# Seven ring places in the output stage, diagonals in place of scaled rows, and a final gain applied slice by slice, in a two-block fp32 transformer kernel

## What is computed

```python
h_l = modulate(rms_norm(x, norm1_w), sh1, sc1)
g_a, g_b = split(sigmoid(h @ w_gate + b_gate), 2)
mix_l = (g_a * (ya @ w_proj_gla) + g_b * (yb @ w_proj_diff)) @ w_out
x_new = x + g1 * mix_l
h2_l = modulate(rms_norm(x_new, norm2_w), sh2, sc2)
x_new = x_new + g2 * conv_ffn(h2_l, w_up, conv_w, conv_b, w_down)
```

## Time and profile before

| what | value |
|---|---|
| runs | 2488.26, 2486.78, 2485.66 us; median 2486.78 |
| profiled execution | 2486.4 us, its span 2484.4 us |
| granted TensorE clock, mean | 0.972 |
| busy: TensorE matmul / weight load | 2363.7 us (95%) / 2074.9 us (84%) |
| busy: VectorE / ScalarE | 1464.6 us (59%) / 1056.2 us (43%) |
| DMA | 456.46 MB, mean 184 GB/s |

### The profile page before, as it was taken

One profiled execution on the slowest core, in us unless ns is written; L12 is line 12 of the kernel. 1 busy time (PEld: TensorE's weight loads), 2 busy tenths in 40 slices (PEclk: granted clock), 3 DMA queues, 4 the chain that ended last, 5 costly groups with the idle time before them and its releaser, 6 DMA issues.

```text
span 2484.4 us, 37594 instructions
## 1 busy us (share of the span) xinstructions
PE 2363.7 (95%) x15615; PEld 2074.9 (84%) x15615; DVE 1464.6 (59%) x2035; ACT 1056.2 (43%) x1435; POOL 43.4 (2%) x53
## 2 busy tenths in 40 slices
PE   5779899999999998898999999999999999999997
PEld 1346787799988998778999988999978999998876
DVE  1124666649567567766888754566766543276654
ACT  3223333345456552335444433444454443254433
POOL 2000000002000000000000000000000000000000
PEclk8889999999999999999999999999999999899999
DMA  9664576645444467775877756666655566244454
GB/s 312 212 206 136 178 220 213 194 136 147 129 145 128 133 208 251 259 241 149 253 243 252 234 189 190 186 180 185 186 164 189 166 192 189 74 130 119 111 174 147
DMA packets 255433, 456.46 MB, mean 184 GB/s; under 512 B 20947, under 2 KB 49937, under 8 KB 254112
## 3 DMA queue, kind: packets, MB, share of 16 engines
q1 hardware_dynamic: 252672, 442.47, 58.0%
q0 software_dynamic: 2016, 7.40, 0.8%
q10 hardware_dynamic: 576, 4.19, 0.4%
HBM read 451.91 MB, written 2.10 MB: 183 GB/s over the span
## 4 chain that ended last, share of the span: by engine, by line
PE 84%; DMA 5%; DVE 5%; ACT 3%; issue 1%; DVEq 1%; ACTq 0%; SPq 0%
PE psum L595 73%; DMA sbuf<-in_w_ada 2%; PE psum L662 2%; PE psum L572 2%; DVE fast L1844 2%; ACT fast L1246 1%; PE psum L1099 1%; DVE sbuf L1892 1%; DMA sbuf<-in_w_proj_diff 1%; DMA sbuf<-in_w_out 1%; PE psum L843 1%; DMA sbuf<-in_w_proj_gla 1%; PE psum L898 1%; PE psum L1129 1%; PE psum L917 1%
## 5 line engine op out<-in xcount | busy, mean ns | idle before, releaser
L595 PE MATMUL psum<-fast,fast 128*128 128x256 f32 (+3 forms) x13680 | 2084.9, 314 | 40.2 <-DVE fast L1844 32.8
L595 PEld LDWEIGHTS psum<-fast,fast 128*128 128x128 f32 (+2 forms) x13680 | 1893.0, 191 | 219.3 <-issue 47.7
L1844 DVE TENSOR_TENSOR fast<-sbuf,fast 128x1024 fp32r<-128x1024 f32 (+3 forms) x655 | 781.4, 1197 | 791.5 <-ACT fast L1246 783.7
L1246 ACT ACTIVATE fast<-sbuf 128x1024 fp32r<-128x1024 f32 (+3 forms) x659 | 678.8, 1034 | 1080.1 <-PE psum L595 918.3
L1892 DVE SCALAR_TENSOR_TENSOR sbuf<-sbuf,sbuf 128x512 f32<-128x512 f32 x240 | 180.4, 752 | 21.6 <-DMA sbuf<-in_w_ada 1.5
L1246 ACT ACTIVATE sbuf<-psum 128x512 f32<-128x512 f32 (+5 forms) x216 | 99.6, 484 | 190.0 <-PE psum L662 90.4
L662 PE MATMUL psum<-sbuf 128*32 128x512 f32 x256 | 70.6, 738 | 27.5 <-DMA sbuf<-in_w_ada 27.4
L572 PE MATMUL psum<-sbuf,sbuf 128*128 128x128 f32 (+2 forms) x317 | 56.9, 291 | 22.2 <-DMA sbuf<-in_consts 10.2
L572 PEld LDWEIGHTS psum<-sbuf,sbuf 128*128 128x128 f32 (+2 forms) x317 | 38.9, 147 | 44.6 <-issue 15.0
L662 PEld LDWEIGHTS psum<-sbuf 128*32 128x32 f32 x256 | 9.8, 118 | 69.3 <-DMA sbuf<-in_w_ada 58.4
L1864 DVE TENSOR_TENSOR fast<-sbuf,fast 128x512 fp32r<-128x512 f32 (+1 forms) x61 | 53.4, 876 | 4.6
(11 more groups left out here) (246 smaller groups left out, 967.7 us busy)
## 6 DMA issues: line engine op xcount, KB each, us to landing
sbuf<-in_w_ada SPq DMA_DIRECT2D x192, 512.0 KB, 4.7
sbuf<-in_w_up SPq DMA_DIRECT2D x176, 512.0 KB, 4.0
sbuf<-in_w_in SPq DMA_DIRECT2D x158, 512.0 KB, 3.9
sbuf<-in_w_down SPq DMA_DIRECT2D x88, 512.0 KB, 4.4
sbuf<-in_w_gate SPq DMA_DIRECT2D x64, 512.0 KB, 3.7
sbuf<-in_w_out SPq DMA_DIRECT2D x64, 512.0 KB, 4.8
sbuf<-in_w_proj_gla SPq DMA_DIRECT2D x16, 512.0 KB, 4.9
sbuf<-in_w_proj_diff SPq DMA_DIRECT2D x16, 512.0 KB, 5.6
```

The source lines that it names most:

```text
L595: last = mm(out, lhsT, rhs, start=first and key not in opened, stop=end, skip_group_check=True)
L1246: return A(out, in_, ACT.Copy, scale=scale)
L1844: last = tt(lo, raw, hi.bitcast(F32), ALU.subtract)
```

## The change

1. **Ring.** Besides the four places, three more exist for the chunks from gate7's first to uv1's last, at M_Y + 18080, 19104 and 21152. Each chunk takes the place that was used least recently. The first load into a new place waits for `diff_pv_done` = 8.
2. **Rows turned by a diagonal.** `rows_scale` goes. `row_scales` multiplies the identity (128 x 128) by the column of factors, once for each half of the rows; `turn_unit` uses these two diagonals as moving operand of an ordinary matmul, with x1 (or the memory rows) unscaled. The scaled copy `xs` goes.
3. **Logarithm early.** Before the last squares of out3, downb3 and o23, ScalarE computes a logarithm of one column that nobody reads.
4. **The end.** In each of the four slices VectorE multiplies x by the gain (two operations of 128 x 512); after `rsqrt`, VectorE scales the first 128 rows and ScalarE the other 128, in four pieces each. The stores keep their order and wait for the engine that makes the piece.

```diff
+EXTRA = [("gate7", "uv1", [18080, 19104, 21152], ("diff_pv_done", 8))]
...
+        self.places = [(0, len(self.chunks), M_RAW + SLOT_WORDS * s, None) for s in range(SLOTS)]
+        for first, final, offsets, free in EXTRA:
+            self.places += [(self.job[first][0], self.job[final][-1] + 1, M_Y + at, free) for at in offsets]
+        self.place, self.earlier, self.loads = [], [], []
+        users = [[] for _ in self.places]
+        for g in range(len(self.chunks)):
+            s = min((n for n, (a, b, _, _) in enumerate(self.places) if a <= g < b),
+                    key=lambda n: users[n][-1] if users[n] else -1)
+            self.place.append(s)
+            self.earlier.append(users[s][-1] if users[s] else None)
+            users[s].append(g)
+            self.loads.append(len(users[s]))
...
-        xs = Y(13984, 2, D)
+        scales = Y(6144, 2, P)
...
-                if g >= SLOTS:
-                    name, count = st.released(g - SLOTS)
+                if st.earlier[g] is not None:
+                    name, count = st.released(st.earlier[g])
+                    sp.wait_ge(S(name), count)
+                elif st.places[st.place[g]][3]:
+                    name, count = st.places[st.place[g]][3]
                     sp.wait_ge(S(name), count)
...
-                sp.wait_ge(S("out_ready"), n + 1)
+                sp.wait_ge(S(f"out_scaled{n % 2}"), n // 2 + 1)
...
             def turn_unit(name, src, u, before):
-                pe.wait_ge(S(f"{name}_rows_scaled"), u // 2 + 1)
+                pe.wait_ge(S(f"{name}_scales_ready"), 1)
...
-                        last = transposed(bank(4 + u % 4, j * T + t * P, P), src[t][:, k * P:(k + 1) * P])
+                        last = mm(bank(4 + u % 4, j * T + t * P, P), src[t][:, k * P:(k + 1) * P], scales[:, t, :],
+                                  start=True, stop=True)
...
+            def logarithms_next():
+                A(small[:, 84:85], small[:, 7:8], ACT.Ln)
...
             rsqrt(small[:, 58:60])
+            act.drain()
+            for n in range(4):
+                act.wait_ge(S("rows_gained"), 2 * n + 2)
+                c = slice(512 * n, 512 * n + 512)
+                copy(onat[:, 1, c], onat[:, 1, c], small[:, 59:60]).then_inc(S("out_scaled1"), 1)
...
-            def rows_scale(name, dst, src, rs):
+            def row_scales(name, rs, earlier=None):
                 rsqrt_wait()
-                for c in range(0, D, 512):
-                    for t in range(2):
-                        last = ts(dst[t][:, c:c + 512], src[t][:, c:c + 512], small[:, rs + t:rs + t + 1], None, ALU.mult)
-                    last.then_inc(S(f"{name}_rows_scaled"), 1)
-                    yield
+                if earlier:
+                    dve.wait_ge(S(f"{earlier}_turned"), 8)
+                for t in range(2):
+                    last = ts(scales[:, t, :], C("ident"), small[:, rs + t:rs + t + 1], None, ALU.mult)
+                last.then_inc(S(f"{name}_scales_ready"), 1)
...
                     stt(x1[:, t, c], src, 0.5, x1[:, t, c], ALU.mult, ALU.add).then_inc(emptied, 1)
+                dve.drain()
+                dve.wait_ge(S("gain_loaded"), 16)
+                for t in range(2):
+                    tt(onat[:, t, c], x1[:, t, c], fgb[:, c], ALU.mult).then_inc(S("rows_gained"), 1)
             row_variance(48, 4, ("x1_squared", 24))
             rsqrt_wait()
-            dve.wait_ge(S("gain_loaded"), 16)
             for n in range(4):
                 c = slice(512 * n, 512 * n + 512)
-                for t in range(2):
-                    stt(onat[:, t, c], x1[:, t, c], small[:, 58 + t:59 + t], fgb[:, c], ALU.mult, ALU.mult
-                        ).then_inc(S("out_ready"), 1)
+                ts(onat[:, 0, c], onat[:, 0, c], small[:, 58:59], None, ALU.mult).then_inc(S("out_scaled0"), 1)
```

More of the change, by code:

```diff
@@ L256, in landed @@
     def landed(self, g):
-        return f"slot_loaded{g % SLOTS}", 16 * (g // SLOTS + 1)
+        return f"slot_loaded{self.place[g]}", 16 * self.loads[g]
     def released(self, g):
@@ L358, in ring @@
             w, row, kt, kp, col, width = st.chunks[g]
-            s = g % SLOTS
-            return area(M_RAW + s * SLOT_WORDS, SLOT_WORDS)[0:kp, 0:kt * width].rearrange("p (k n) -> p k n", k=kt)
+            return area(st.places[st.place[g]][2], SLOT_WORDS)[0:kp, 0:kt * width].rearrange("p (k n) -> p k n", k=kt)
         def half(g, part):
@@ L991, in turn_unit @@
                         k = 2 * u + j
-                        last = transposed(bank(4 + u % 4, j * T + t * P, P), src[t][:, k * P:(k + 1) * P])
+                        last = mm(bank(4 + u % 4, j * T + t * P, P), src[t][:, k * P:(k + 1) * P], scales[:, t, :],
+                                  start=True, stop=True)
                 last.then_inc(S(f"{name}_turned"), 1)
-            xsT = [xs[:, 0, :], xs[:, 1, :]]
+            x1T = [x1[:, 0, :], x1[:, 1, :]]
             pe.wait_ge(S("g1_kept"), 4)
             for u in range(4):
-                turn_unit("norm2", xsT, u, 0)
+                turn_unit("norm2", x1T, u, 0)
             def norm2_chunk(q):
@@ L1002, in norm2_chunk @@
                 if q >= 1 and q + 3 < 8:
-                    turn_unit("norm2", xsT, q + 3, 0)
+                    turn_unit("norm2", x1T, q + 3, 0)
             def up(i):
@@ L1040, in norm3_units @@
                 for u in range(8):
-                    turn_unit("norm3", xsT, u, 16)
+                    turn_unit("norm3", x1T, u, 16)
                     yield
@@ L1599, in squares @@
                       ).then_inc(S("x1_squared"), 1)
+            def logarithms_next():
+                A(small[:, 84:85], small[:, 7:8], ACT.Ln)
             for n in range(4):
                 steps(f"out{n}")
+                if n == 3:
+                    logarithms_next()
                 squares(0, n)
@@ L2221, in unit @@
                 split_values(hi, lo, X[:, lc, 1, 2 * u:2 * u + 2, :]).then_inc(S(f"{name}_ready"), 1)
-            x1T, xsT = ([x[:, 0, :], x[:, 1, :]] for x in (x1, xs))
             row_variance(48, 4, ("x1_squared", 8))
[L2225 to L2232, removed]
+            row_scales("norm2", 58)
+            for u in range(3):
+                unit("norm2", u, 0, 0)
             def taps(s, i, b):
@@ L2302, in mem_units @@
                 yield
[L2303 to L2306, removed]
+                row_scales("mem", 66, "norm2")
+                for _ in range(7):
+                    yield
                 for u in range(8):
@@ L2318, in norm3_units @@
                 row_variance(48, 4, ("x1_squared", 16))
-                scaling = rows_scale("norm3", xsT, x1T, 58)
                 yield
[L2321 to L2326, removed]
+                row_scales("norm3", 58, "mem")
+                yield
+                for u in range(8):
                     yield
```

## The result

The changed kernel takes 2472.87 us (median of 7 runs, 2468.39 to 2480.11); the kernel before took 2488.15 us on the same chip (7 runs). The ratio is 0.9938, 95% interval 0.9924 to 0.9953: faster by 15 us where 28 were forecast, and 4 us above the upper end of the range. The profiled execution took 2468.4 us with a span of 2466.3 us.

What follows compares the result with a forecast made beforehand. The output stage was held by the latency of a four-place ring, not bandwidth. Gains 25.0 + (0.4 + 1.2 + 0.4) + 0.8 + 0.5 = 28.3 us off 2486.4 gave 2458.1, forecast as 2458.5 us; range 2450 to 2469.

Steps and rivals of the forecast that it cites:

- The diagonals: Turns at norm2, mem and norm3: an fp32 product takes 0.11 us like a transpose, so cost zero.
- rival of more passes: Turns: an fp32 matmul takes twice a transpose, adding 10.6 us over 96 operations, 2469 us in all; chance 0.04.
- The ring: Output stage (pg, pd, out): three more places for weight loads end most waits, 25.0 us gained.
- floor: pd: VectorE's work without its waits for ScalarE allows no less than 49.9 us; 51 was taken.
- the delay behind each panel's end: out: additions and ScalarE's squares after every job delay the next split, 1.7 us in all.
- The 2 us set aside for bursts: Output stage: stalls that remain while loads of x and memory rows compete, 2 us (0 to 11).
- The rival of bursts: Output stage: bursts and late splits keep a third of the stalls, 19 us gained in all, 2468 us; chance 0.18.
- Places idle: Ring: release order leaves the new places unused, only 3.3 us gained, 2483.5 us; chance 0.03.
- slower by SyncE's wait: gate7: SyncE's queue waits for the eighth `diff_pv_done`, holding all loads; for instance 2497 us; chance 0.03.
- Scalings: VectorE's spared scalings shorten TensorE's waits: 0.4 us at norm2, 1.2 at mem, 0.4 at norm3.
- Logarithm early: norm2: the table load moves into ScalarE's wait for the additions, 0.8 us gained; 0 at norm3.
- The end: Last slice: the first store goes out 0.5 us earlier; the stores' DMA time still ends last.

Runs made afterwards that it cites:

- e3: The kernel before with only the row scaling replaced by diagonals: 2497.07 us, ratio 1.0033.
- e1: The changed kernel without the diagonals (rows scaled first, turned by transposes; ring, early logarithm and new end kept): 2462.11 us, ratio 0.9891 to the kernel before.
- e2: The kernel before with only the three further ring places: 2464.26 us, ratio 0.9902.
- e8: e1 with half of VectorE's w_ada sums in the output stage left out: 2456.62 us, ratio 0.9878 to the kernel before.
- e9: e1 with each pd panel's two tiles worked off one by one behind the next panel's first two chunks: 2462.63 us, ratio 0.9899 to the kernel before.
- e10: e9 with the same reorder for the additions of out0 to out2: 2460.97 us, ratio 0.9885 to the kernel before.
- e5: e1 with each piece turned by a product with the identity instead of a transpose: 2473.8 us, ratio 0.9944 to the kernel before.
- e11: e1 repeated unchanged as yardstick for the two reorders: 2461.47 us, ratio 0.9890 to the kernel before.
- e6: e1 with one further ring place instead of three: 2468.29 us, ratio 0.9917 to the kernel before.

## Why the prediction was wrong, step by step

**The diagonals: the step that failed.** The prediction said that "nearest in kind is the fold's fp32 matmul with the identity, also 128 columns, 0.89 / 8 = 0.11 us" and "I take 0.11 and a cost of zero". The divisor was wrong. Line 689 issues four products a fold, in a loop over four blocks, and the row says x8; line 686 issues one and its row says x2. An instruction count in a trace is not a count of products in the source, and both rows of the same group said so beside the transposes' x4 for four. Rightly divided, 0.89 / 4 = 0.22 us, twice the transpose, and 96 x 0.11 = 10.6 us where the sum had nothing. This was my rival of more passes, held at 0.04 because "the rows speak against it". They spoke for it. Measured: 10.75 us in the chain, worked out from norm2's rows for all 24 units, 8.3 us net for e3, which also has the spared scalings, and 10.8 between the medians of e1 and the changed kernel. The Trainium skill, "FP8 and Floating Point Precision", section "TensorE Precision Notes", counts four passes for true fp32. The prediction's estimate from it, 0.21 us for a product, stands beside 0.22 measured; the rows do not show passes, they show two instructions per product, each as long as the whole transpose of the same piece. The rule was right in size here and deserved more than 0.04.

**The ring: right in mechanism, by the traces 2.7 us too high.** Taken as 25.0 us, it is 22.3 us in the traces of the changed kernel and of e2; e2's time, 24.5 us, has an interval of 21 to 28 and cannot tell the two apart. pg 45.1 us (46 forecast) and pd 51.7 (51) came near, and VectorE is nearly full in pd, busy 44.9 of 51.7 us. But 49.9 us was no floor: VectorE still waits 4.0 us for ScalarE, and what its window holds beside that is 47.7 us, because some of its operations now fall outside it (57 instead of 60). That pd came to 51.7 is in part luck. out was mis-sized, 98.4 us instead of 94. I gave 1.7 us to the delay behind each panel's end; the waits there are 2.77 us at out0, 1.55 and 0.37 after. I had left out that out0 begins behind the two tiles of pd3. The timeline, VectorE and TensorE:

```profile
1003.96 0.43 DVE L1895 CAST fast<-sbuf 128x512 fp32r<-128x512 f32 x1
1004.46 0.69 DVE L1897 TENSOR_TENSOR fast<-sbuf,fast 128x512 fp32r<-128x512 f32 x1
1005.07 2.35 DVE L1877 TENSOR_TENSOR fast<-sbuf,fast 128x1024 fp32r<-128x1024 f32 x2
...
1006.43 0.56 PE L612 MATMUL psum<-fast,fast 128*128 128x512 f32 x1 [2.77 <-DVE fast L1877]
```

ScalarE's copy was ready at 1004.81 and VectorE took it at 1005.07, then the product followed. With half the sums (e8) this wait is still 1.96 us, so it is VectorE's load in part and in part its order. The gap is paid twice, as the windows of TensorE's clock (the number after POOL's) in the gap and behind it show:

```profile
1003.60:1006.40 2.80, 0.06 (x1) 0.00 (x0) 2.65 (x5) 1.06 (x1) 0.00 (x0) 1.00 1.03 418
1006.40:1007.40 1.00, 0.97 (x3) 0.81 (x4) 1.00 (x1) 0.00 (x0) 0.00 (x0) 0.64 1.01 418
1007.40:1009.40 2.00, 2.00 (x7) 1.51 (x6) 1.81 (x4) 0.00 (x0) 0.00 (x0) 0.50 0.95 343
1009.40:1010.40 1.00, 1.00 (x5) 0.81 (x4) 0.85 (x1) 0.00 (x0) 0.00 (x0) 0.66 0.87 315
1010.40:1011.40 1.00, 1.00 (x6) 0.82 (x5) 0.00 (x0) 0.29 (x1) 0.00 (x0) 1.00 0.91 334
```

For some 3 us the clock is at its lower level, 1.2 GHz: 0.36 + 2 x 0.5 + 0.34 = 1.7 us of full-speed work lost. Now out adds up: TensorE is busy 93.7 us, of which 1.7 are lost clock, so 92.0 of full-speed work, 4.7 of waits and 1.7 of clock are 98.4. That the forecast had 92.3 for the work is luck too: it counted three folds, and only two lie in out, so by its own pace it should have been 90.5; the 32 chunks took some 0.05 us more than 2.72 each. The 2 us set aside for bursts were not needed for bursts: no wait for a load is left in the stage of the changed kernel. The rival of bursts does not hold there, although its time, 2468, came nearer than my forecast; only in e9 and e10, with VectorE's order eased, does a burst reach TensorE.

**Places idle, and slower by SyncE's wait:** neither. The prediction held that the wait would be over before gate7's first load was due. It was not: that load was due earlier now, and the queue stood 1.8 us for the signal in the changed kernel and in e1, e2 and e5 to e11 alike. The stage after it has the same six waits of TensorE in e1, e2, e5 and the changed kernel: the chunks in hand cover it, as the prediction said for that case.

**Scalings:** 2.0 us taken. The waits of TensorE fell by 0.4 us at norm2 (6.34 in e1 to 5.93), by 0.8 at the memory rows (1.2 taken) and by 0.4 at norm3 (1.74 to 1.34): 1.6 us. The term was about right, and it is a seventh of what the turns cost.

**Logarithm early:** 0.8 us, measured 0.83 (7.17 to 6.34). **The end:** 0.5 us, measured 5.32 - 4.73 = 0.6. Only the exponential's table is loaded after the variance; the early load did not bring it along.

**The sum with the measured terms,** the stage by the windows: 22.3 + 1.6 + 0.8 + 0.6 - 10.75 = 14.6 us, and the medians say 15.3. The two profiled executions lie 18.0 us apart, but some 3.1 us of that are in the first 860 us, ahead of the change; the other 14.9 fit the sum. The sum differs from the 28.3 forecast by 13.7 us: 10.75 for the turns, 2.7 for the ring and some 0.3 for the rest.

## What to carry to other kernels

Before a product is priced from a row of the trace, divide its time by the number of products that the source issues, not by the row's count: in these traces an fp32 product of 128 columns stands as two instructions and 0.22 us, an fp32 transpose as one and 0.11 us, so a turn by a diagonal costs twice a transpose and pays only where the scaling it saves holds TensorE up for more than 0.45 us for four pieces. This ring, held by latency, was nearly cured by one further place; after that look at the engine that releases the places, because its load and what its order puts in front of a release are the next bound. And a rival that has a written rule for it should be tested against the source line, not only against a quotient.

## What the runs showed that was not expected

- A short gap can cost as much again in clock. After TensorE's waits of 2.77 us here (1006.43) and 2.61 us in e6 (971.19) the granted clock went to the 1.2 GHz level within a microsecond and stayed there for about 3 us, though TensorE was busy again. In e6 at 971.19:

```profile
971.20:973.00 1.80, 1.80 (x12) 1.80 (x13) 1.68 (x3) 0.00 (x0) 0.00 (x0) 0.78 0.33 90
973.00:975.00 2.00, 2.00 (x11) 2.00 (x11) 2.00 (x2) 0.00 (x0) 0.00 (x0) 0.50 0.79 208
975.00:977.00 2.00, 2.00 (x17) 2.00 (x16) 1.60 (x3) 1.06 (x1) 0.00 (x0) 0.85 0.77 229
```

- The length of the gap does not decide it alone. The clock also fell behind waits of 2.15 us (1049.91 in the kernel before) and 2.49 us (1012.02 in e9), and behind e6's second gap, 2.78 us at 1013.92, it was at 0.50 for about 6 us (24.85 us for 96 products, where e8 took 22.03 at 1.00). It stayed at 1.00 behind 1.55 us here, 1.96 us in e8 (1005.71), 2.55 us in e3 (1100.62) and 2.45 us in e10, whose window behind the gap is:

```profile
1012.80:1013.80 1.00, 0.96 (x4) 0.85 (x5) 1.00 (x1) 0.44 (x1) 0.00 (x0) 1.00 1.04 385
```

What decides it was not tried.
